# SSD decays from running sums stored as rows and read back for all partitions by DMA, with two of five gate pieces moved into the tile loop

## The chip, the cores and the metric

One core of a Trainium2 chip runs the whole program. The metric is the device time of one execution in microseconds (us), and the number quoted is the median of several runs. The engines are TensorE (PE, with its weight load PEld), VectorE (DVE), ScalarE (ACT), GpSimd (POOL) and the sequencer SyncE (SP), which here only issues DMAs. They run side by side and wait for one another through semaphores.

## The reference

One layer of a streaming encoder in f32: 512 prompt tokens and 8 streams of 16 sample tokens, 640 tokens in all, width 1024. A Mamba-2 branch (SSD) and a sparse attention branch work on the same normed input, are gated and merged, and a mixture of 32 experts follows. The change is in the SSD branch. For each head it needs, over a tile of 128 tokens (a chunk),

```python
a_cum = jnp.cumsum(ak, axis=1)                       # ak = dt * A, one number per token and head
seg = a_cum[:, :, None] - a_cum[:, None, :]
decay = jnp.where(causal, jnp.exp(jnp.where(causal, seg, 0.0)), 0.0)
cb = jnp.einsum('blgn,bsgn->blsg', ck, bk)
y = jnp.einsum('blsg,blsgr,bsgrp->blgrp', cb, decay, xk)
y = y + jnp.einsum('blgn,bgrpn,blgr->blgrp', ck, state, jnp.exp(a_cum))
...
y_ssd = rmsnorm(y_ssd * jax.nn.silu(z), ssm_norm_g)  # over all 2048 channels
```

There are 32 heads in 4 groups of 8. The sum of squares for the last norm runs over all four groups.

## The kernel before

**Tiling.** 640 tokens are five tiles of 128 (`NT` = 5; tiles 0 to 3 prompt, tile 4, `SMP`, the eight streams). The SSD branch runs group by group, g = 0 to 3 (`ssd_pe`, `ssd_act`, `ssd_dve`, and the loops in the GpSimd and SP blocks). Each engine has its own program in a fixed order, written out by hand; what order results between engines comes from semaphores. PSUM has 8 banks of 128 x 512. `plan_banks` and `plan_group` give each use of a bank a key such as ("z", g, j) and take the banks of a pool in turn: `lo` is banks 0 to 3, `hi` 4 to 7. TensorE may fill a bank (`claim`) when its earlier user has read it (`release`), so with four banks in turn each key waits for the reader of the fourth key before it in its pool.

**A group on TensorE** (`ssd_pe`): six products for x, B and C over the prompt (`xbc` 0 to 5, each eight 128 x 128 weights by 512 columns), with the sample tokens' part `xbcS`; between them in the first group the running sums `ac` and totals `ae`, in later groups the squares of the group before (`squares_pe`: ones times zT, four products for the prompt and four for the sample, summed over partitions and channels at once); then the gate products `z` 0 to 3 and, for the sample tokens of all four, `zS`; transposes of the convolution's last rows (`cO`) and of B (`bt`); and the tile loop. The loop has six steps. Step s transposes x of tile s (`xt`), makes C B^T (`cb`) and the segment sums (`sg`, lines 868 to 874: eight matmuls, one per head, whose weights are one column of a broadcast over 128 columns, so that the running sum of the head stands in every partition), and for tile s-1 the state's part (`yi`, line 882), the new state (`st`, line 890) and the output (`yo`, line 896). After it come the eight streams' states (`so`, `s0`, `sn`, `ys`).

**A group on ScalarE** (`ssd_act`): for each of the six products a copy into `raw` (two buffers) and, one step later, the silu of VectorE's convolution result; the silus of z into zT (lines 1328 to 1332); copies of cO and bt; then for each tile eight Relu (line 1352: the running sum of a head minus its value at the own token, in mt), two Exp over mt (line 1358) and four half Exp of the running sums into ebs (lines 1367 and 1368), both from the PSUM bank of `sg`. After the loop: copies of states, the squares of the gated output into zT (line 1380), and the norm's gain (line 1383).

**A group on VectorE** (`ssd_dve`): for each of the six products the convolution (lines 1556 and 1558), with rounds of the attention's top-k between (lines 1963 and 1964); in the fourth of the six also `squares_dve` of the group before (line 1675: sums added into ssrow). In the loop: dt times x (1588), cb times the causal mask (1593), the state and output sums of the tile before (`tile_dve`), and mt times cb (1602).

**GpSimd** copies the convolution's last rows, multiplies xdt by weights (`xw`, line 737), masks B by stream (743), and issues the DMAs of results: conv rows, states (759), and the group's output to `y_spill` (762).

**SP** issues the loads. Weights go through a ring of three slots (`chunks`): a slot is loaded anew when its user, named in `ring.add`, is done; for wz that is `zS`. In a group SP issues, in order, the conv rows, the weights up to wz of the next group, and four loads of 512 KB of states (line 575). At the end of the stage SP waits for the last squares and reloads q (line 586) for the attention. DMAs of one queue are issued in the order of the program; a wait in front of one holds all behind it.

Of the kernel before, what the change touches and what calls it, by code (L numbers as in the profile page):

```python
# [19 lines left out]
P = 128  # L20
# [173 lines left out]
def plan_group(b, g):  # L194
# [18 lines left out]
    b.add(("zS", g), hi)  # L213
# [24 lines left out]
    if g == GROUPS - 1:  # L238
        for c in range(4):
            b.add(("ga", 0, c), lo)  # L240
            if c == 1:
                for i in range(2):
                    b.add(("ss", g, i), hi)
# [3 lines left out]
def hybrid_layer(nc, x_prompt, x_sample, cache_k, cache_v, cache_kidx, state_conv, state_ssm,  # L247
# [39 lines left out]
    with ExitStack() as ctx:  # L287
# [94 lines left out]
        sout = xdt[:, 1, :]  # L382
        cin, cst = a2.take(6, P), a2.take(6, 24)
# [54 lines left out]
        q_spill = nc.dram_tensor("q_spill", (P, KD, TP), F32, kind="Internal").ap()  # L438
        y_spill = nc.dram_tensor("y_spill", (P, 16, T), F32, kind="Internal").ap()
# [44 lines left out]
        def wait_chunk(pe, key):  # L484
# [7 lines left out]
            "ident_ready", "pads_zeroed", "x_squares", "x_var", "x_std", "x_scaled",  # L492
            "a_row_ready", "wl_ready", "wsel_ready", "rel_used",
            "bias_ready", "dt_exp", "a_exp", "a_ready", "raw_zeroed", "raw_ready", "conv_done",
            "xs_ready", "gathered", "bms_ready", "mt_size", "mt_exp", "xw_ready", "mt_ready",
            "y_gated", "y_squares", "y_gained",
            "q_spilled", "y_spilled", "crow_written", "sout_written", "q_back", "vnew_loaded", "y_back",
            "router_loaded", "fin_loaded", "at_exp", "kz_ready", "p_scaled", "ss_var", "ss_std", "m_ready", "hx_squares",
            "hx_var", "hx_std", "hx_scaled", "r_exp_in", "r_exp", "hot_ready", "rows_ready", "at_ready", "at_used",
            "t_full", "t_read", "up_full", "silu_ready", "he_ready", "heT_full", "heT_ready",  # L500
            "dn_full", "dn_read", "xn_stored", "fx_squares", "fx_var", "fx_std",
            "fin_ready", "last_ready", "rms_ready", "fx_scaled", "y_written", "parts_added", "last_chain")}
        w13_loaded = [sem(f"w13_loaded{i}") for i in range(XS)]
        st0_loaded = [sem(f"st0_loaded{i}") for i in range(3)]
        st0_written = [sem(f"st0_written{i}") for i in range(3)]
        w2_loaded = [sem(f"w2_loaded{i}") for i in range(XS)]
# [13 lines left out]
        def _(sp):  # L520
# [41 lines left out]
            for g in range(GROUPS):  # L562
# [6 lines left out]
                chunks(("wz", min(g + 1, GROUPS - 1)) if g + 1 < GROUPS else ("wgb", 0))  # L569
# [11 lines left out]
            wait_read(sp, ("ss", GROUPS - 1, 1))  # L581
# [74 lines left out]
        def _(pool):  # L656
# [59 lines left out]
            for g in range(GROUPS):  # L716
# [39 lines left out]
                for j in range(4):  # L756
# [3 lines left out]
                                   st0[:, u % 3, :, :]).then_inc(st0_written[u % 3], 16)  # L760
                pool.wait_ge(S["y_gained"], g + 1)
# [1505 lines left out]
```

## Time and profile before

| | us |
|---|---|
| median of 3 runs | 1826.1 (1823.59 to 1828.19) |
| the profiled execution | 1830.48 |
| its span in the trace | 1828.7 |
| TensorE busy | 1635.3 |
| VectorE busy | 688.4 |
| ScalarE busy | 457.1 |
| GpSimd busy | 174.7 |

The profile describes one execution on one core. Busy time is summed over the span; what matters for a change is which engine the others wait for in the stage that it touches. A row of a timeline merges neighbouring instructions of a kind: start, duration, engine, line of the kernel, what is written and read, how many, and in brackets the idle time before it and what ended it. An f32 matmul shows as two records. The mean granted clock of TensorE was 0.94 of full speed. The four SSD groups lie between about 213 and 848 us of the span.

### The profile page before, as it was taken

How to read it: one execution, taken by the hardware profiler on the slowest of the kernel's cores; microseconds unless marked ns; L12 is line 12 of the kernel's file. 1: busy time of each engine (PE TensorE's matmuls, PEld its weight loads, DVE VectorE, ACT ScalarE, POOL GpSimd, SP SyncE). 2: the span in 40 equal slices, each digit the busy share in tenths (PEclk: the TensorE clock that was granted, in tenths of full speed). 3: DMA queues.
4: the chain of work that ended last, by engine and by line, in shares of the span. 5: the costliest groups of instructions: out<-in, count | busy, mean ns of one | idle time of the engine just before them, and what ended most of it. 6: DMA issues, size and time to landing. Idle time of an engine off the chain costs nothing. (4 is left out here: it accounts for less than half of the span.)

```text
span 1828.7 us, 19455 instructions
## 1 busy us (share of the span) xinstructions
PE 1635.3 (89%) x7752; PEld 1004.3 (55%) x7752; DVE 688.4 (38%) x1371; ACT 457.1 (25%) x1070; POOL 174.7 (10%) x250
## 2 busy tenths in 40 slices
PE   8998999999899899989998899999999967977770
PEld 5555555755664764655666665655564544544440
DVE  3003283776677469453554450010001243111105
ACT  2005322521621621522554330000000100111112
POOL 4000000200200210120000000000000012322212
PEclk9999999999999999988999999999999977988985
DMA  9010312220322224024003434031223166999964
GB/s 237 23 46 24 128 47 80 80 87 23 101 78 68 83 94 127 1 65 134 1 1 82 116 138 139 1 138 46 47 75 136 35 261 243 414 416 415 414 251 173
DMA packets 109936, 231.67 MB, mean 127 GB/s; under 512 B 30236, under 2 KB 56420, under 8 KB 101012
## 3 DMA queue, kind: packets, MB, share of 16 engines
q1 hardware_dynamic: 98772, 199.28, 31.3%
q0 software_dynamic: 11072, 31.12, 4.8%
q8 instruction: 63, 1.03, 0.2%
q14 instruction: 29, 0.24, 0.0%
HBM read 200.77 MB, written 31.56 MB: 127 GB/s over the span
## 5 line engine op out<-in xcount | busy, mean ns | idle before, releaser
L1044 PE MATMUL psum<-hT,wring 128*128 128x512 f32 (+1 forms) x2176 | 598.3, 439 | 0.0
L1044 PEld LDWEIGHTS psum<-hT,wring 128*128 128x128 f32 x2176 | 335.7, 196 | 258.3 <-issue 258.0
L1048 PE MATMUL psum<-ident,arena 128*128 128x128 f32 (+3 forms) x926 | 148.2, 294 | 45.3 <-DVE arena L1724 7.3
L1406 ACT ACTIVATE arena<-psum 128x512 f32<-128x512 f32 (+7 forms) x200 | 109.4, 569 | 278.3 <-PE psum L1044 168.4
L1048 PEld LDWEIGHTS psum<-ident,arena 128*128 128x128 f32 (+3 forms) x926 | 112.4, 155 | 100.3 <-issue 66.4
L1044 PE MATMUL psum<-arena,wring 128*128 128x512 f32 (+1 forms) x512 | 138.8, 433 | 0.0
L1044 PEld LDWEIGHTS psum<-arena,wring 128*128 128x128 f32 x512 | 77.0, 190 | 61.6 <-issue 61.6
L1255 PE MATMUL psum<-wring,arena 128*64 128x256 f32 x608 | 79.0, 418 | 23.9 <-issue 17.8
L1255 PEld LDWEIGHTS psum<-wring,arena 128*64 128x64 f32 x608 | 52.0, 151 | 46.4 <-issue 24.4
L1202 PE MATMUL psum<-wring,arena 128*128 128x512 f32 x160 | 72.4, 613 | 3.8 <-DVE arena L2022 3.8
L1700 DVE CUSTOM_DVE_ANT_0 arena<-psum,arena 128x256 f32<-128x256 f32 (+3 forms) x64 | 46.6, 729 | 67.9 <-PE psum L960 42.9
L2064 DVE TENSOR_TENSOR arena<-psum,arena 128x128 f32<-128x128 f32 x32 | 9.3, 292 | 165.0 <-ACT arena L1534 152.1
L1044 PE MATMUL psum<-oT,wring 128*128 128x512 f32 (+1 forms) x256 | 69.6, 434 | 0.0
L1963 DVE MAX8 ssq<-arena 128x8 f32<-128x1040 f32 (+3 forms) x80 | 66.6, 833 | 2.1
L1558 DVE SCALAR_TENSOR_TENSOR arena<-arena,pc 128x664 f32<-128x664 f32 x72 | 65.6, 911 | 2.6
L2010 DVE TENSOR_TENSOR arena<-psum,arena 128x512 f32<-128x512 f32 x8 | 5.5, 692 | 159.2 <-PE psum L1044 159.2
L1964 DVE MATCH_REPLACE8 arena<-ssq,arena 128x1040 f32<-128x1040 f32 (+3 forms) x80 | 65.2, 815 | 0.0
L772 POOL MEMSET arena<- 128x2048 f32 x1 | 1.8, 1804 | 645.8 <-DVE arena L2029 645.8
L1271 PE MATMUL psum<-arena 128*64 128x512 f32 x256 | 60.9, 592 | 0.4 <-ACT arena L1536 0.4
L1393 ACT ACTIVATE arena<-psum 128x512 f32<-128x512 f32 x16 | 9.4, 597 | 192.6 <-PE psum L1044 192.6
L1534 ACT ACTIVATE arena<-psum 128x128 f32<-128x128 f32 x32 | 8.9, 277 | 193.2 <-PE psum L1255 180.0
L1044 PEld LDWEIGHTS psum<-oT,wring 128*128 128x128 f32 x256 | 38.8, 191 | 30.6 <-issue 30.6
(324 smaller groups left out, 1928.7 us busy)
## 6 DMA issues: line engine op xcount, KB each, us to landing
wring<-in_w SPq DMA_DIRECT2D x38, 1024.0 KB
arena<-in_w SPq DMA_DIRECT2D x32, 1024.0 KB, 25.5
wring<-in_w_in SPq DMA_DIRECT2D x13, 2048.0 KB, 7.9
hT<-in_w SPq DMA_DIRECT2D x14, 1024.0 KB
oT<-in_w SPq DMA_DIRECT2D x12, 1024.0 KB
arena<-in_state_ssm SPq DMA_DIRECT2D x16, 512.0 KB, 9.1
out<-arena POOLq DMA_DIRECT2D x16, 512.0 KB, 3.9
wring<-in_w_ssm_out SPq DMA_DIRECT2D x4, 2048.0 KB, 14.0
```

Of the source, the lines that this page charges most:

```text
L1044: ins = mm(out, chunk[:, k, m0:m0 + m], rhs(k), start=first and k == 0, stop=last and k == ks - 1)
L1048: return nc.tensor.transpose(out, in_, ident[0:rows, 0:rows])
L1202: ins = mm(o, mrg[:, k, tt * P:(tt + 1) * P], ws[n][:, k, :], start=k == 0, stop=k == KD - 1)
L1255: ins = mm(pbank(2 + e % 2)[h * SLOTS:(h + 1) * SLOTS, 0:FF].rearrange("p (c f) -> p c f", c=2), hgT[:, e % 2, k, :], w13[e % XS][:, :, k, ...
L1271: ins = mm(pbank(4 + e % 2)[m * SLOTS:(m + 1) * SLOTS, :], heT[:, e % 2, k, :], w2s[e % XS][:, k, HD2 * m:HD2 * (m + 1)], start=k == 0, st ...
L1393: release(fn(gate[:, i, j, 0:TP], bank((what, m, j)), ACT.Sigmoid), (what, m, j))
L1406: release(fn(out, in_, ACT.Copy), key)
L1558: ins = stt(out=a, in0=r[:, w:w + 664], scalar=cw_col[:, w, ct:ct + 1], in1=a, op0=ALU.mult, op1=ALU.add)
L1700: release(nc.vector.tensor_tensor_reduce(out=out, in0=scores, in1=bias, scale=-ATT_SCALE, scalar=3.0e38, op0=ALU.add, op1=ALU.min, accum_o ...
L1963: link(nc.vector.max(top8, scores))
L1964: link(nc.vector.match_replace(scores, top8, scores, TAKEN))
L2064: tt_(hetm[:, u % 2], pbank(2 + u % 2)[:, HF:FF], hsil[:, u % 2], ALU.mult).then_inc(S["he_ready"], 1)
```

## The change

The segment sums are made once, in the first group, for all 32 heads as rows (`ar`: heads on partitions, tokens in columns), copied by ScalarE to `arow`, written by DMA to DRAM (`a_rows`), and for each tile of each group read back so that all 128 partitions hold the eight heads' rows (512 KB a tile). They land in `mt`, which with two halves of `raw` for tile 2 makes three places for six halves. ScalarE works on them in place, in a new order: first the half Exps into ebs, then Relu, then Exp. The decays of tiles 0 and 1 are done in the convolution loop (after the fifth and the sixth silu), those of tile 2 ahead of the silu of z3, of tile 3 ahead of that of zS, and of tile 4 last. `z3` is now made in step 0 of the tile loop and `zS` in step 4. SP's weights go up to wbc of the next group, then the five decays, then wz of the next group. The squares are summed over the channels on GpSimd into ssrow, and TensorE sums over the partitions once, at the end of the last group, after the fourth gate product and no longer after the second. Some semaphores are shared (`row_squares`, `row_var`, `row_std`) in place of three sets with the same waits.

```diff
@@ plan_group
-    if g:
-        for i in range(2):
-            b.add(("ss", g - 1, i), hi)
-    else:
+    if g == 0:
         for tt in range(NT):
             b.add(("ac", tt), hi)
             b.add(("ae", tt), hi, readers=2)
+        for i in range(2):
+            b.add(("ar", i), hi)
...
-    for j in range(4):
+    for j in range(3):
         b.add(("z", g, j), lo)
-    b.add(("zS", g), hi)
...
-            for i in range(2):
-                b.add(("sg", g, step, i), hi)
+        if step == 0:
+            b.add(("z", g, 3), lo)
+        elif step == NT - 1:
+            b.add(("zS", g), hi)
@@ tiles
+        arow = ebs.rearrange("p u n -> p (u n)")[0:HEADS, 0:T]
+        mt_f = mt.rearrange("p u n -> p (u n)")
+        def decays(tt, i):
+            return raw[:, i, 3:515] if tt == 2 else mt[:, 2 * (tt % 3) + i, :]
+        def decays_load(g, tt):
+            return (2, g) if tt == 2 else (tt % 3, 2 * g + tt // 3)
...
+        a_rows = nc.dram_tensor("a_rows", (NT, HEADS, P), F32, kind="Internal").ap()
@@ SP, in each group
-                chunks(("wz", min(g + 1, GROUPS - 1)) if g + 1 < GROUPS else ("wgb", 0))
+                chunks(("wbc", g + 1) if g + 1 < GROUPS else ("wga", 0))
+                if g == 0:
+                    wait_read(sp, ("ar", 0))
+                    wait_read(sp, ("ar", 1))
+                    sp.dma_start(a_rows.rearrange("t h l -> h t l"), arow.rearrange("h (t l) -> h t l", t=NT)) \
+                        .then_inc(S["arow_written"], 16)
+                    sp.wait_ge(S["arow_written"], 16)
+                for tt in range(NT):
+                    if tt == 2:
+                        sp.wait_ge(S["conv_done"], 6 * (g + 1))
+                        sp.wait_ge(S["gathered"], 6 * (g + 1))
+                    elif tt > 2:
+                        wait_full(sp, ("yo", g, tt - 3))
+                    elif g:
+                        wait_full(sp, ("yo", g - 1, tt + 3))
+                    at = (tt % 3) * 1024
+                    dst = raw[:, :, 3:515] if tt == 2 else mt_f[:, at:at + 1024].rearrange("p (i n) -> p i n", i=2)
+                    sp.dma_start(dst, a_rows[tt, HG * g:HG * (g + 1), :].rearrange("(o i h) l -> o i (h l)", o=1, i=2)
+                                 .broadcast_to([P, 2, 512])).then_inc(decays_loaded[decays_load(g, tt)[0]], 16)
+                chunks(("wz", g + 1) if g + 1 < GROUPS else ("wgb", 0))
...
-            wait_read(sp, ("ss", GROUPS - 1, 1))
+            sp.wait_ge(S["squares_added"], GROUPS)
@@ GpSimd, in each group, after the states' writes and ahead of y_spill
+                pool.wait_ge(S["y_squares"], g + 1)
+                for j in range(4 if g else 3):
+                    a, b = (ssrow, zT[:, j, :]) if g else (ssrow if j else zT[:, 0, :], zT[:, j + 1, :])
+                    ins = nc.gpsimd.tensor_tensor(ssrow, a, b, ALU.add)
+                    if j < (3 if g else 2):
+                        link(ins)
+                ins.then_inc(S["squares_added"], 1)
@@ ssd_pe
-            if g:
-                squares_pe(pe, g - 1)
-            else:
+            if g == 0:
...
+                for i in range(2):
+                    o = claim(pe, ("ar", i))
+                    for tt in range(4 * i, min(4 * i + 4, NT)):
+                        ins = mm(o[0:HEADS, (tt - 4 * i) * P:(tt - 4 * i + 1) * P], av[:, tt, :],
+                                 (cum_p if tt < SMP else cum_s)[:], start=True, stop=True)
+                    filled(ins, ("ar", i))
...
-            for j in range(4):
+            for j in range(3):
                 o = claim(pe, ("z", g, j))
...
-                    for i in range(2):
-                        o = claim(pe, ("sg", g, tt, i))
-                        for h in range(4):
-                            hd = HG * g + 4 * i + h
-                            ins = mm(o[:, h * P:(h + 1) * P], av[:, tt, hd:hd + 1].broadcast_to([P, P]),
-                                     (cum_p if tt < SMP else cum_s)[:], start=True, stop=True)
-                        filled(ins, ("sg", g, tt, i))
                 if step == 0:
+                    o = claim(pe, ("z", g, 3))
+                    filled(product(o, w, 3 * P, P, prompt, TP), ("z", g, 3))
                     continue
+                if step == NT - 1:
+                    o = claim(pe, ("zS", g))
+                    for j in range(4):
+                        ins = product(o[:, j * P:(j + 1) * P], w, j * P, P, sample, P)
+                    filled(ins, ("zS", g))
...
-            pe.wait_ge(S["y_squares"], g + 1)
+            pe.wait_ge(S["squares_added"], g + 1)
...
-                for j in range(4):
-                    ins = mm(o[:, 0:b - a], ones[:], zT[:, j, a:b], start=j == 0, stop=j == 3)
-                filled(ins, ("ss", g, i))
+                filled(mm(o[:, 0:b - a], ones[:], ssrow[:, a:b], start=True, stop=True), ("ss", g, i))
@@ ssd_act
+                if j >= 5:
+                    decays_act(act, g, j - 5, fn)
             if g:
-                wait_full(act, ("ss", g - 1, 1))
-            for j in range(4):
+                act.wait_ge(S["squares_added"], g)
+            for j in range(3):
                 wait_full(act, ("z", g, j))
...
+            decays_act(act, g, 2, fn)
+            wait_full(act, ("z", g, 3))
+            release(fn(zT[:, 3, 0:TP], bank(("z", g, 3)), ACT.Silu), ("z", g, 3))
+            decays_act(act, g, 3, fn)
+            wait_full(act, ("zS", g))
+            release(fn(zT[:, :, TP:T], bank(("zS", g)).rearrange("p (j q) -> p j q", j=4), ACT.Silu), ("zS", g))
+            decays_act(act, g, 4, fn)
...
+        def decays_act(act, g, tt, fn):
+            k = NT * g + tt
+            b, n = decays_load(g, tt)
+            act.wait_ge(decays_loaded[b], 16 * (n + 1))
+            if tt >= 2:
+                wait_read(act, ("yo", g, tt - 2))
+            elif g:
+                wait_read(act, ("yo", g - 1, tt + 3))
+            for i in range(2):
+                dst = ebs[:, k % 2, 2 * i * P:2 * (i + 1) * P].rearrange("p (j l) -> p j l", l=P)
+                src = decays(tt, i).rearrange("p (j o l) -> p o j l", o=2, l=P)
+                fn(dst[0:HP], src[0:HP, 0], ACT.Exp)
+                ins = fn(dst[HP:P], src[HP:P, 1], ACT.Exp)
+            ins.then_inc(S["ebs_ready"], 1)
+            act.wait_ge(S["ebs_ready"], k + 1)
+            for i in range(2):
+                for h in range(4):
+                    hd = HG * g + 4 * i + h
+                    m = decays(tt, i)[:, h * P:(h + 1) * P]
+                    ins = fn(m, m, ACT.Relu, bias=acv[:, tt, hd:hd + 1], scale=-1.0)
+                ins.then_inc(S["mt_size"], 1)
+            for i in range(2):
+                act.wait_ge(S["mt_size"], 2 * k + i + 1)
+                m = decays(tt, i)
+                fn(m, m, ACT.Exp, scale=-1.0).then_inc(S["mt_exp"], 1)
```

## Rows read from the trace of the kernel before

**Rows 1.** The page's first part: busy time of each engine, share of the span, instructions.

```profile
PE 1635.3 (89%) x7752; PEld 1004.3 (55%) x7752; DVE 688.4 (38%) x1371; ACT 457.1 (25%) x1070; POOL 174.7 (10%) x250
```

**Rows 2.** Timeline of TensorE, third group: start, us, engine, line, operation, count, [idle before].

```profile
546.92 4.49 PE L947 MATMUL psum<-arena,ones 128*128 128x512 f32 x16
...
611.46 1.16 PE L872 MATMUL psum<-cum_p,arena 128*128 128x128 f32 x8 [2.94 <-ACT arena L1368]
...
619.85 1.09 PE L896 MATMUL psum<-arena 128*64 128x128 f32 x16
...
621.59 1.95 PE L872 MATMUL psum<-cum_p,arena 128*128 128x128 f32 x16
623.38 1.06 PE L882 MATMUL psum<-arena 128*128 128x128 f32 x8
...
625.22 1.09 PE L896 MATMUL psum<-arena 128*64 128x128 f32 x16
...
634.99 1.98 PE L896 MATMUL psum<-arena 128*64 128x128 f32 x16 [3.30 <-DVE arena L1602]
```

**Rows 3.** Timeline of ScalarE, third group.

```profile
585.97 0.72 ACT L1322 ACTIVATE arena<-arena,pc 128x512 f32<-128x512 f32 x1 [10.15 <-DVE arena L1558]
...
589.35 0.60 ACT L1330 ACTIVATE arena<-psum 128x512 f32<-128x512 f32 x1 [1.40 <-PE psum L1044]
...
603.36 0.60 ACT L1332 ACTIVATE arena<-psum 128x512 f32<-128x512 f32 x1 [6.55 <-PE psum L1044]
...
606.12 2.17 ACT L1352 ACTIVATE arena<-psum,arena 128x128 f32<-128x128 f32 x8 [0.77 <-PE psum L872]
608.31 1.28 ACT L1358 ACT_TABLE_LOAD   x1
...
622.68 2.17 ACT L1352 ACTIVATE arena<-psum,arena 128x128 f32<-128x128 f32 x8 [0.75 <-PE psum L872]
```

**Rows 4.** Groups of VectorE's instructions: count, busy us, mean ns, idle before.

```profile
L1602 DVE TENSOR_TENSOR arena<-arena 128x512 f32<-128x512 f32 x40 | 25.7, 685 | 17.8 <-ACT arena L1358 17.8
```

**Rows 5.** Timeline of VectorE, third group.

```profile
562.47 1.00 DVE L1675 TENSOR_TENSOR arena<-arena,psum 128x512 f32<-128x512 f32 x2
```

**Rows 6.** Windows: us, busy of each engine, then PE's clock, DMA share, GB/s.

```profile
633.00:640.50 7.50, 5.51 (x30) 4.69 (x31) 3.10 (x5) 1.79 (x3) 3.07 (x6) 0.54 0.07 19
```

**Rows 7.** Timeline of ScalarE, first and second group.

```profile
276.82 0.60 ACT L1406 ACTIVATE arena<-psum 128x512 f32<-128x512 f32 x1 [3.66 <-PE psum L1044]
...
311.35 0.60 ACT L1332 ACTIVATE arena<-psum 128x512 f32<-128x512 f32 x1 [6.55 <-PE psum L1044]
...
442.42 0.72 ACT L1322 ACTIVATE arena<-arena,pc 128x512 f32<-128x512 f32 x1 [14.62 <-DVE arena L1558]
...
456.18 0.60 ACT L1332 ACTIVATE arena<-psum 128x512 f32<-128x512 f32 x1 [6.55 <-PE psum L1044]
```

**Rows 8.** DMA issues of 563 to 583 us: count, KB each, median us to landing.

```profile
wring<-in_w_in SPq DMA_DIRECT2D x2, 512.0 KB, 4.6
```

**Rows 9.** DMA issues of the whole span.

```profile
arena<-in_x_prompt SPq DMA_DIRECT2D x8, 512.0 KB, 4.0
```

**Rows 10.** Groups of GpSimd's instructions.

```profile
L737 POOL TENSOR_TENSOR arena<-arena 128x512 f32<-128x512 f32 x20 | 20.8, 1041 | 220.9 <-DVE arena L1588 220.9
```

**Rows 11.** Timeline of ScalarE at the end of the fourth group.

```profile
819.24 2.98 ACT L1383 ACTIVATE oT<-oT,pc 128x640 f32<-128x640 f32 x4
```

**Rows 12.** Timeline of TensorE where the attention starts.

```profile
848.51 0.83 PE L960 MATMUL psum<-arena,oT 128*128 128x128 f32 x6
```

**Rows 13.** DMA issues of 600 to 625 us.

```profile
wring<-in_w_in SPq DMA_DIRECT2D x1, 2048.0 KB, 7.8
arena<-in_state_ssm SPq DMA_DIRECT2D x3, 512.0 KB, 9.2
```

**Rows 14.** Groups of ScalarE's instructions.

```profile
L1352 ACT ACTIVATE arena<-psum,arena 128x128 f32<-128x128 f32 x160 | 43.5, 383 | 11.5 <-PE psum L872 11.3
```

More of the change, by code:

```diff
@@ L505, in hybrid_layer @@
         st0_written = [sem(f"st0_written{i}") for i in range(3)]
+        decays_loaded = [sem(f"decays_loaded{i}") for i in range(3)]
         w2_loaded = [sem(f"w2_loaded{i}") for i in range(XS)]
@@ L834, in ssd_pe @@
             w = wait_chunk(pe, ("wz", g))
-            for j in range(4):
+            for j in range(3):
                 o = claim(pe, ("z", g, j))
                 filled(product(o, w, j * P, P, prompt, TP), ("z", g, j))
-            o = claim(pe, ("zS", g))
-            for j in range(4):
-                ins = product(o[:, j * P:(j + 1) * P], w, j * P, P, sample, P)
-            filled(ins, ("zS", g))
             pe.wait_ge(S["gathered"], 6 * (g + 1))
@@ L1297, in ssd_act @@
                     fn(w2v, w2v, ACT.Exp).then_inc(S["a_exp"], 1)
+                    copy(("ar", 0), arow[:, 0:512], bank(("ar", 0))[0:HEADS, :])
+                    copy(("ar", 1), arow[:, 512:T], bank(("ar", 1))[0:HEADS, 0:P])
+                if j == 0 and g:
+                    wait_full(act, ("yo", g - 1, 2))
                 if j < 6:
@@ L1325, in ssd_act @@
                        bias=cb_col[:, ct:ct + 1]).then_inc(S["xs_ready"], 1)
+                if j >= 5:
+                    decays_act(act, g, j - 5, fn)
             if g:
-                wait_full(act, ("ss", g - 1, 1))
-            for j in range(4):
+                act.wait_ge(S["squares_added"], g)
+            for j in range(3):
                 wait_full(act, ("z", g, j))
                 release(fn(zT[:, j, 0:TP], bank(("z", g, j)), ACT.Silu), ("z", g, j))
-            wait_full(act, ("zS", g))
-            release(fn(zT[:, :, TP:T], bank(("zS", g)).rearrange("p (j q) -> p j q", j=4), ACT.Silu), ("zS", g))
             if g:
@@ L1385, in ssd_act @@
             if g == GROUPS - 1:
+                act.wait_ge(S["squares_added"], GROUPS)
                 gate_act(act, "ga", 0, fn)
+        def decays_act(act, g, tt, fn):
[21 more added lines that the diff above has]
+                act.wait_ge(S["mt_size"], 2 * k + i + 1)
+                m = decays(tt, i)
+                fn(m, m, ACT.Exp, scale=-1.0).then_inc(S["mt_exp"], 1)
         def gate_act(act, what, m, fn):
@@ L1568, in ssd_dve @@
                         release(tt_(w2v[:, tt, :], bank(("ae", tt))[:, 0:HEADS], acv[:, tt, :], ALU.subtract), ("ae", tt))
-                if j == 3 and g:
-                    squares_dve(dve, g - 1)
                 a, b = TOP_UPTO[g], TOP_UPTO[g + 1]
@@ L1600, in ssd_dve @@
                         dve.wait_ge(S["mt_exp"], 2 * k + i + 1)
-                        m = mt[:, (2 * k + i) % 4, :].rearrange("p (h l) -> p h l", h=4)
+                        m = decays(tt, i).rearrange("p (h l) -> p h l", h=4)
                         tt_(m, m, cbs[:, k % 2, :].rearrange("p (o l) -> p o l", o=1).broadcast_to([P, 4, P]), ALU.mult) \
@@ L1604, in ssd_dve @@
             k = NT * g + SMP
-            for i in range(2):
-                wait_read(dve, ("sg", g, SMP, i))
+            dve.wait_ge(S["ebs_ready"], k + 1)
             wait_read(dve, ("yo", g, SMP))
@@ L1642, in tile_dve @@
                 wait_full(dve, ("yi", g, tt))
-                for i in range(2):
-                    wait_read(dve, ("sg", g, tt, i))
+                dve.wait_ge(S["ebs_ready"], k + 1)
                 wait_read(dve, ("yo", g, tt - 1))
@@ L1671, in squares_dve @@
                 src = bank(("ss", g, i))[:, 0:b - a]
-                if g == 0:
-                    ins = nc.vector.tensor_copy(ssrow[:, a:b], src)
-                else:
-                    ins = tt_(ssrow[:, a:b], ssrow[:, a:b], src, ALU.add)
-                release(ins, ("ss", g, i))
+                release(nc.vector.tensor_copy(ssrow[:, a:b], src), ("ss", g, i))
                 wait_read(dve, ("ss", g, i))
```

81 lines of the change are left out of this document (26 added, 55 removed).

## The prediction

> **What bounds the kernel now.** The page's first part comes first: TensorE is busy 89% of the span, every other engine under 40% [rows 1]. So I read the change from TensorE's side, in the four SSD groups, which it alone touches (about 213 to 848 us). The timeline of TensorE in the third group (g = 2) shows why that stage is TensorE's: its rows follow one another without idle time except for 2.94 us at the first tile and 3.30 us at the last [rows 2]. A middle tile costs 5.37 us from one L896 group to the next (619.85 to 625.22), of which the segment sums (L872) hold 1.79 us (621.59 to 623.38) [rows 2]. ScalarE waits 0.75 us a tile for L872 [rows 3], so its own work (eight Relu, two Exp, four half Exp) is 5.37 - 0.75 = 4.6 us. VectorE has seven operations of 0.69 us a tile [rows 4] and a smaller one, about 5 us. Three engines are therefore nearly level inside the tile loop, and taking work from one of them cannot give its full price.
>
> **What is removed.** 160 segment-sum matmuls, eight a tile in 16 records (621.59 [rows 2]): 20 tiles by 1.79 us is 35.8 us. The squares: a row of 4.49 us a group (546.92 [rows 2]), of which 0.17 overlaps with its neighbour, so 4.32, and 17.3 us in all; two matmuls (about 1.0 us: four records, two of 0.43 and two of 0.11) stay at the very end. Added on TensorE: five 32-row running sums, 128 columns each, about 1.2 us once by the spacing in L872. Net 50.9 us of TensorE work. That is the upper bound; what follows is how much of it ScalarE's new order gives back.
>
> **The third group, step by step, on the trace's own clock.**
> (1) When the loop can start. Before it needed z(0..3) and the sample part; two of these five, z3 and zS, now lie inside the loop. They are 14.0 us (589.35 to 603.36 [rows 3]). With 4.3 us of squares gone, TensorE comes to the transposes at 603.2 - 18.3 = 584.9. But these wait for the last silu of the convolution, which started on ScalarE at 585.97 [rows 3], when VectorE's convolution ended (it has top-k rounds between its six parts). That VectorE chain starts at the first product of the group and doesn't shorten, except for 1.0 us of adding squares [rows 5]. So the silu ends at 585.0 + 1.1 = 586.1. Up to here the removed squares are worth nothing: another engine is late.
> (2) The first hand-over. ScalarE now does the decays of tile 1 right after this silu, and only then z0, z1, z2 and the copies of cO and B. The bank of cb(0) is free when cO(0) has been copied (four banks in turn: cO0, cO1, bt0, bt1, cb0), and that of z3 when z0 has been read. In front of it: a load of the Exp table 1.28 [rows 3], the decays 4.75 (the 4.6 of a tile, with 0.15 for a new wait on its own half Exps), a load of the Silu table 1.28, three silus 1.6, the copy 0.6: 586.1 + 9.5 = 595.6. TensorE is there at 587.5. It stands idle for 8.1 us, where before it had 2.94.
> (3) Then xt/cb and z3. z3 is 6.87 us at full clock. After an idle time of only 3.3 us the granted clock was 0.54 over 633 to 640.5 [rows 6], that is mostly at 1.2 GHz; after 8 us I expect the same. Over such a stretch the loss is between 1.7 and 3.4 us by how much of 7.5 us was slow; I take 2.3. z3 ends at 605.0.
> (4) Tiles 0 to 2. Step 1 is 2.7 us on TensorE (xt, cb, state, output, from the rows of 0.95 to 1.1 us [rows 2]): 607.7. VectorE reads that output (0.7), and only then may ScalarE begin tile 2: 608.4 + 4.75 = 613.2. VectorE has 1.3 (tile 1's product), 1.0, four operations of 0.69 and 1.3 more: 614.7. The output of tile 2 is done at 615.6. The steps are now VectorE's 5 us, not TensorE's 3.6: the 1.79 us saved per tile is given back here but for 0.4.
> (5) Tile 4. xt, cb and zS on TensorE: 615.6 + 0.7 + 7.15 = 623.5. TensorE then has tile 3 (2.9 us) and is out of work at 626.4. ScalarE must turn zS (0.6), load the Exp table (1.28), do the half Exps, Relus and the first Exp of tile 4 (4.2), VectorE the product (0.7): 630.2. So 3.8 us idle, in place of the 3.30. The output takes 1.98 us at the slow clock, as in the row of before: 632.2, against 634.99 + 1.98 = 636.97 [rows 2]. **Saved: 4.8 us** of a removed 8.9 + 4.3 us.
>
> **The other groups.** The fourth I take like the third: 4.8. In the second the last silu stands only 13.8 us before zS's (442.42, 456.18 [rows 7]) against 17.4 in the third [rows 3]: everything in (2) to (5) hangs on it, so 3.6 less: 1.2. In the first the silu is early, but the running sums go out to DRAM and come back: SP issues the write behind the 1 MB of the next B and C weights, when their slot is free (the product read at 276.82 [rows 7], 278.0 with the added matmuls). Their 4.6 us to landing [rows 8], 2.7 for the write (80 KB, an estimate below the 4.0 of a 512 KB load [rows 9]) and 4.0 for the first load give 289.3 for tile 0's decays, 294.0 for their end, 296.3 for the last silu, and by the sum of (2) 305.8 for cO. From there 36.6 us as in the third: 342.4, against 311.35 [rows 7] + 33.6 = 345.0 (33.6 is the third group's way from zS's silu to 636.97). Saved 2.6.
>
> **The end.** GpSimd adds four 128 x 640 parts. Its row of 1041 ns for 512 elements a partition [rows 10] puts one at 1.3, four at 5.2 us. In the first three groups they fall into VectorE's idle time after the gated product. In the last the squares are done when the gain starts, 819.24 [rows 11], the sum at 824.5, and TensorE has gates to do until 837: hidden. y_spill, now behind the adds, and with it q's reload, come about 1 us later than in the trace; the attention starts at 848.5 - 3.3 = 845.2 [rows 12], and a 2 MB load from 829.5 with 7.8 us to landing [rows 13] leaves 8 us for VectorE's two short copies of the keys. 17.3 less 1.0 on paper, 3.3 here.
>
> **What is hidden.** Twenty more loads of 512 KB. Tile 2's comes after the last convolution and is wanted 20 us later; tile 3's is issued at 607.7 and wanted at 616, tile 4's 4 us later and wanted at 625. A 512 KB load of states took 9.2 us even behind 2 MB [rows 13]; alone I take the 4.0 of the x rows. Bounds: nothing, and 5 us once in the first group if a broadcast load takes 8. The loads that they displace matter more: z's weights for the next group (slot free only when zS is done) now stand before the states on SP's queue. 2 MB took 7.8 us to land [rows 13] and I put the first state 2 us later: 623.5 + 9.8 = 633.3, wanted at 633.1 (after the 0.9 us of state transposes). Cost zero now; up to 4 us a group if the loop goes quicker than I sum.
>
> **The sum.** 2.6 + 1.2 + 4.8 + 4.8 + 3.3 = 16.7 us. The profiled execution took 1830.48 us, 4.4 above the median of 1826.1; its stages after 848 us shift whole. 1830.5 - 16.7 = 1813.8; at the median, 1809.4.
>
> **A rule on the tables.** ScalarE pays 1.28 us a load in the trace, and nothing else: the Relus end at 606.12 + 2.17 = 608.29, the load starts at 608.31 [rows 3]. By the trace's price a group has four loads on the path, 5.1 us, already in the sum. The Trainium skill, "ScalarE: Activation LUTs", What ACT_TABLE_LOAD costs, adds about 1.38 us of drain to every switch, and its rule to batch by table set speaks against this change, which goes from Silu to Exp five times a group where it went once. By the page's figure the drains would be 5.5 us a group more, 22 in all: 1831 as an estimate. The row shows no such gap.
>
> **Rivals.**
> A, TensorE stays the bound: the waits of (2) and (5) don't arise because ScalarE is far enough ahead. For it: ScalarE is busy only 25% of the span [rows 1]. Against: its order is serial. 50.9 us less: 1775.
> B, ScalarE's serial piece is longer than I sum; this one ends slower. Place: the decays of tile 1 ahead of cO's copy, and those of tile 4 after zS. Price: a Relu alone lasts 383 ns [rows 14] and eight come to 3.1 instead of 2.17; with two half-clock stretches of full length (1.1 more each) and the waits between the three sub-steps at 0.5 each, 6.0 us a group (1.8, 2.2 and 2.0), 24 in all: 1833. It makes the kernel slower than before from 4.2 us a group on.
> C, a switch of tables costs twice its row, because the engine must run empty first and the loads of before stood where that didn't show: four more times 1.28 a group, 20.5 us: 1830. Against it: the load of 608.31 stood in a full stretch and had no gap [rows 3].
> D, the exchange is even: the idle time grows by just what was removed, or the reloaded rows in the first group and the states behind z's weights take back 12 us: 1821 to 1830.
>
> **Chances.** My forecast 0.54 (own range 1800 to 1819); A or half of it 0.12; B 0.16; C 0.04; D 0.14. The range 1791 to 1830 leaves out A's far end and most of B. A measurement of this kernel tells 0.3% (5.5 us) from no change: faster is my forecast and A, 0.66; same C and D, 0.18; slower B, 0.16.
>
> **What would show it.** TensorE idle for about 8 us ahead of the first cb or z3 in groups 2 to 4, released by ScalarE; a second idle time of about 4 us before the last tile's output; steps of 5 us in between with VectorE full; L872 gone; ten table loads a group; the squares' sum of GpSimd done before the gates are. Wrong if TensorE runs through (A), if the state transposes wait for DMA, or if the last silu of the convolution isn't what ends the wait before the loop.

## The result: 1.3% slower, 1848.8 us against 1825.4, and the profile after

| | before | after |
|---|---|---|
| median, four runs each on one chip | 1825.44 (1823.59 to 1828.19) | 1848.8 (1847.72 to 1852.39) |
| the profiled execution | 1830.48 | 1852.39 |
| its span | 1828.7 | 1850.6 |

The ratio is 1.0127, 95% interval [1.0109, 1.0146]. I had predicted 1809.4 us in a range of 1791 to 1830: the wrong direction, and outside the range. The first part of the page of after answers to [rows 1]:

```profile
span 1850.6 us, 18747 instructions
PE 1591.5 (86%) x7382; PEld 961.8 (52%) x7382; DVE 683.1 (37%) x1365; ACT 509.8 (28%) x1104; POOL 194.3 (10%) x265
```

TensorE is busy 43.8 us less than in [rows 1] and the span is 21.9 us longer: its idle time grew by 65.7 us. The waits of TensorE by line and releaser, in total, times, longest, of after:

```profile
PE psum L917 <- ACT arena L1381: 34.6, 4, 8.6
PE psum L902 <- ACT arena L1451: 29.9, 4, 8.7
PE psum L931 <- DVE arena L1645: 19.2, 4, 4.8
```

Each of the three comes once a group. L902 (cb of tile 0) and L931 (output of tile 4) are the two waits that the prediction has, at 8.1 and 3.8 us. The largest, L917, the state's part `yi` of tile 1, it doesn't have. (`yi` is what the state that earlier tiles left adds to a tile's output.) The timeline of TensorE of after in the third group, against [rows 2]:

```profile
601.30 1.20 PE L1081 MATMUL psum<-ident,arena 128*128 128x128 f32 x9 [0.34 <-ACT arena L1360]
611.17 0.79 PE L902 MATMUL psum<-arena 128*128 128x128 f32 x2 [8.66 <-ACT arena L1451]
611.75 8.94 PE L1077 MATMUL psum<-hT,wring 128*128 128x512 f32 x16
...
622.14 1.09 PE L931 MATMUL psum<-arena 128*64 128x128 f32 x16
...
632.69 2.05 PE L917 MATMUL psum<-arena 128*128 128x128 f32 x8 [8.64 <-ACT arena L1381]
634.53 1.79 PE L925 MATMUL psum<-arena 128*128 128x512 f32 x2
...
637.99 1.06 PE L917 MATMUL psum<-arena 128*128 128x128 f32 x8
638.88 1.02 PE L925 MATMUL psum<-arena 128*128 128x512 f32 x2
...
641.58 7.31 PE L1077 MATMUL psum<-hT,wring 128*128 128x128 f32 x64
...
656.48 1.95 PE L931 MATMUL psum<-arena 128*64 128x128 f32 x16 [4.80 <-DVE arena L1645]
```

z3 (611.75) is done at 620.7. Why is its silu (L1381) so late? The timeline of ScalarE of after says it:

```profile
610.54 1.49 ACT L1451 ACTIVATE arena<-psum 27x512 f32<-27x512 f32 x4
624.12 1.28 ACT L1418 ACT_TABLE_LOAD   x1 [12.10 <-DVE oT L1704]
...
627.15 2.45 ACT L1426 ACTIVATE arena<-arena 128x128 f32<-128x128 f32 x8
629.50 1.13 ACT L1431 ACTIVATE arena<-arena 128x512 f32<-128x512 f32 x2
630.65 1.28 ACT L1381 ACT_TABLE_LOAD   x1
631.95 0.60 ACT L1381 ACTIVATE arena<-psum 128x512 f32<-128x512 f32 x1
```

In ScalarE's program the decays of tile 2 stand ahead of the silu of z3. They overwrite ebs, so they wait for VectorE's read of yo(0), the copy in L1704. ScalarE stands idle for 12.10 us, the last 3.4 of them with z3 ready, then does table load, decays and table load, and only at 632.55 is the bank of z3 free. The keys of the low banks go in turn z3, xt1, yo0, xt2, yi1: the next user of z3's bank is yi(1). So tile 1's state part waits for the silu of a gate piece whose result is wanted only behind the loop. Then it and the row behind it run at half speed: 2.05 and 1.79 us where the same rows a step later take 1.06 and 1.02. The windows of after, with the granted clock behind the busy times, show 0.53 there, that is the 1.2 GHz level, after 8.64 us of idle time; z3 behind the first idle time had 0.76:

```profile
611.00:620.50 9.50, 9.33 (x18) 4.32 (x19) 1.59 (x3) 1.02 (x4) 0.00 (x0) 0.76 0.00 0
632.50:636.30 3.80, 3.61 (x12) 2.26 (x12) 0.69 (x1) 0.04 (x1) 0.00 (x0) 0.53 0.00 0
```

The price is 8.64 us of idle time and 0.99 + 0.77 us of slow rows, 10.4 us a group and 41.6 in all. With the 16.7 us of saving that I had summed this makes +24.9 us, against +21.9 in the profiled execution.

The end of the stage, of after: GpSimd's sum of squares, and then, on TensorE's timeline, the two products over the partitions and the start of the attention, which answers to [rows 12]:

```profile
842.13 5.49 POOL L793 TENSOR_TENSOR arena<-arena 128x640 f32<-128x640 f32 x4 [8.71 <-ACT arena L1397]
```

```profile
859.88 1.24 PE L981 MATMUL psum<-arena,ones 128*128 128x512 f32 x4
...
868.11 0.83 PE L993 MATMUL psum<-arena,oT 128*128 128x128 f32 x6
```

### The profile page after: what moved, and what is told of

It reads as the page before. It is cut to its first block and busy times, and to the rows that moved or that the text cites. A ratio compares the mean times of both kernels' runs of the same rounds, so it can differ in the third digit from the quotient of the medians.

```text
span 1850.6 us, 18747 instructions
## 1 busy us (share of the span) xinstructions
PE 1591.5 (86%) x7382; PEld 961.8 (52%) x7382; DVE 683.1 (37%) x1365; ACT 509.8 (28%) x1104; POOL 194.3 (10%) x265
## 5 line engine op out<-in xcount | busy, mean ns | idle before, releaser
L1451 ACT ACTIVATE arena<-psum 128x512 f32<-128x512 f32 (+5 forms) x202 | 109.8, 568 | 239.4 <-PE psum L1077 140.4
```

The costliest lines, as they stand in the source:

```text
L1451: release(fn(out, in_, ACT.Copy), key)
```

## Experiments

Theory T: the loss is a chain: VectorE's read of yo(0), then the decays of tile 2, then the silu of z3, then the bank for yi(1). Rivals: the table loads (R1), the reloads from DRAM and other traffic (R2), the decays as such being too much serial work on ScalarE (R3). Each ratio is to the kernel before on the same chip. The rows come from several chips, so compare ratios and not medians. The last three columns are of each kernel's one profiled execution: the length of the SSD stage, from the transposes of the first convolution rows (212.84 in before) to the start of the attention (848.51); the length of the attention over the prompt behind it, from the first to the last of the products of [rows 12]; and the table loads of ScalarE in the stage.

| kernel | median us | ratio [95%] | stage us | attention us | table loads |
|---|---|---|---|---|---|
| before | 1825.44 | 1 | 635.7 | 118.7 | 9 |
| e4, squares alone | 1807.33 | 0.9885 [0.9863, 0.9907] | 621.3 | 110.4 | 9 |
| e3, squares and rows, gates before the loop | 1777.82 | 0.9713 [0.9673, 0.9754] | 587.3 | 110.4 | 25 |
| after | 1848.8 | 1.0127 [1.0109, 1.0146] | 654.0 | 118.7 | 41 |
| e1, after, silu of z3 ahead of decays 2 | 1820.24 | 0.9951 [0.9934, 0.9969] | 626.4 | 118.7 | 33 |
| e5, after, decays 2 without their wait | 1806.84 | 0.9864 [0.983, 0.9897] | 617.8 | 110.4 | 41 |
| e2, e1 and decays 1 behind z0 to z2 | 1784.43 | 0.9763 [0.9742, 0.9784] | 588.5 | 118.7 | 33 |
| e6, e2 and silu of zS last | 1779.76 | 0.9717 [0.9686, 0.9748] | 585.6 | 118.7 | 26 |
| e7, e6 and states ahead of z's weights | 1762.47 | 0.9626 [0.9597, 0.9655] | 565.1 | 118.7 | 26 |
| e9, e7 and decays 2 without their wait | 1761.79 | 0.9632 [0.9613, 0.965] | 565.5 | 118.7 | 26 |
| e8, e3 and decays 2 without their wait | 1777.24 | 0.9691 [0.9653, 0.9728] | 585.7 | 118.8 | 25 |
| e10, e8 and states ahead of z's weights | 1768.75 | 0.9655 [0.9618, 0.9691] | 581.7 | 118.7 | 25 |

The attention is not touched by any edit, and yet it has two lengths. From 5 us after its start TensorE runs for 20 us at a granted clock of 0.50 (1.2 GHz) in nine of these executions, and at 1.00 (2.4 GHz) in those of e3, e4 and e5. The windows of e2 and of e3, whose attention starts at 802.40 and 802.45 us behind the same kind of products and has the same 2.35 us of idle time near its start:

```profile
807.40:827.40 20.00, 20.00 (x65) 11.28 (x66) 8.38 (x50) 8.66 (x38) 0.00 (x0) 0.50 0.01 2
807.45:827.45 20.00, 18.70 (x96) 11.58 (x96) 12.56 (x69) 13.11 (x53) 0.00 (x0) 1.00 0.01 2
```

What decides between the two isn't known. So some 8 us, 0.45% of the time, can lie between two kernels' ratios without a cause in the change; the stage's length is free of it, but it is from one execution of each.

**e1: the order of two calls on ScalarE.**

```diff
-            decays_act(act, g, 2, fn)
             wait_full(act, ("z", g, 3))
             release(fn(zT[:, 3, 0:TP], bank(("z", g, 3)), ACT.Silu), ("z", g, 3))
+            decays_act(act, g, 2, fn)
```

> The changed kernel with two blocks of ScalarE's program exchanged: the silu of z3 stands ahead of tile 2's decays. Theory (the bank): z3 and yi(1) share a PSUM bank, z3 is read only after tile 2's decays, and these wait for tile 0's output to be read, so TensorE stands 8.6 us before yi(1) in each group and runs on at the slow clock for about 2 us. Then this wait goes, yo(2) waits 1 to 2 us instead, and a group is 9 us shorter: 1811 us (1805 to 1817). Rival 1 (ScalarE's decays and table loads as a whole are the bound, yi(1) is only the first place where it shows): the wait moves to yo(2), 3 us a group at most: 1837. Rival 2 (the rows read back by DMA arrive late): no difference, 1849.

The wait of L917 for z3's bank is gone, with as many reloads as in after. The table loads are not as many: with the silu out from between them, the decays of tiles 2 and 3 follow each other on one table, 33 loads for 41. The eight that are gone are 10.3 us at most, so this run alone does not settle R1; e5 does. TensorE in the third group of e1:

```profile
588.03 1.20 PE L1081 MATMUL psum<-ident,arena 128*128 128x128 f32 x9 [0.34 <-ACT arena L1360]
597.89 0.80 PE L902 MATMUL psum<-arena 128*128 128x128 f32 x2 [8.66 <-ACT arena L1451]
...
615.34 1.16 PE L917 MATMUL psum<-arena 128*128 128x128 f32 x8 [0.66 <-DVE arena L1695]
...
618.11 1.17 PE L931 MATMUL psum<-arena 128*64 128x128 f32 x16 [0.75 <-DVE arena L1645]
...
634.82 1.97 PE L931 MATMUL psum<-arena 128*64 128x128 f32 x16 [4.80 <-DVE arena L1645]
```

From the first transpose to the end of the last output it is 48.8 us (588.03 to 636.79), in after 57.1 (601.30 to 658.43). The two ratios differ by 0.0176, 32 us; the stage is 27.6 us shorter. At 1820 us the kernel is still some 9 us slower than I expected of it, and outside the range given. ScalarE in e1:

```profile
607.78 0.60 ACT L1380 ACTIVATE arena<-psum 128x512 f32<-128x512 f32 x1 [9.03 <-PE psum L1077]
611.17 1.28 ACT L1418 ACT_TABLE_LOAD   x1 [2.79 <-DVE oT L1704]
```

The silu of z3 runs as soon as z3 is there, and the wait for yo(0) is still 2.79 us long behind it.

**e5: the other link of the same chain.** Tile 2's decays don't wait for VectorE; the silu of z3 stays behind them. The wait guards the half Exps of tile 0, and these have no reader: a prompt starts without a state, so there is no yi of tile 0 (VectorE copies its output where it adds for the others). It can go without a race.

```diff
-            if tt >= 2:
+            if tt >= 3:
                 wait_read(act, ("yo", g, tt - 2))
-            elif g:
+            elif g and tt < 2:
                 wait_read(act, ("yo", g - 1, tt + 3))
```

> The changed kernel, ScalarE's order as it is, but tile 2's decays don't wait for tile 0's output to be read (tile 0 has no part that reads ebs, so the buffer is free). Theory (the bank of z3 is read late because tile 2's decays stand before it and wait): they now run beside z3's product, the silu of z3 follows at once, the 8.6 us before yi(1) go without the exchange of the first experiment; 1814 us (1808 to 1822). Rival (it was the exchange itself, one pair of table loads fewer, that helped): 1840 or more.

The same idle time is gone (none before yi(1); 0.65 us before yi(2), where e1 has 0.66), with all 41 table loads and all reloads of after, and the stage is 36.3 us shorter than that of after: R1 and R2 fall as the cause of the loss. The kernel is faster than e1 by 0.9%, 16 us. Of the 17.0 us between the two profiled executions 8.7 are in the stage, where ScalarE does tile 2's decays in the 9.03 us in which e1 leaves it waiting for z3; 8.3 are the attention's clock. Either link broken ends the loss: it is the chain, not the order alone and not the wait alone.

**e4 and e3: the parts without the gate pieces.** e4 is before with GpSimd's sum of squares alone. e3 is after with z3 and zS made ahead of the loop again:

```diff
-            for j in range(3):
+            for j in range(4):
                 o = claim(pe, ("z", g, j))
...
+            o = claim(pe, ("zS", g))
...
-                if step == 0:
-                    o = claim(pe, ("z", g, 3))
-                if step == NT - 1:
-                    o = claim(pe, ("zS", g))
```

> The kernel before with the squares' sum alone moved to GpSimd and one product at the end. Theory: ahead of the loop TensorE is the late one here (the last silu is 13 to 17 us early), so all of it counts: 4 times 4.3 less 1.1 is 16.2 us: 1809 us. My prediction's step (1) says that the same edit is worth nothing once the gates are in the loop. Rival (GpSimd's sums delay VectorE or the conv rows, or the convolution bounds already): 1825.

> The changed kernel with z3 and zS back ahead of the tile loop on TensorE and ScalarE (and their banks planned there): only the rows by DMA and the squares on GpSimd remain of the change. Theory: tiles 0 and 1 get their decays beside 14 us of gate products, no bank of a gate stands in the loop, and of 51 us removed from TensorE nearly all is won: 1776 us (1768 to 1788), the loop 23 us instead of 33. Rival (rows by DMA cost what they save: ScalarE's half Exps, Relus and Exps in place last longer, and each load waits for an output three tiles back): 1815 to 1830.

Squares alone are worth 1.15%, about 21 us, but 14.4 us in the stage, for 16.2 expected; its profiled execution had another 8.3 us from the attention's clock, which are not the squares'. That leaves little that the GpSimd adds could cost. Rows and reloads in addition are worth 0.9885 - 0.9713 = 1.7%, 31 us, and 34.0 in the stage, of the 35.8 of matmuls removed. All reloads and all decays of after are in e3, so R2 and R3 fall. The whole loss goes with the two gate pieces: 1.0127 against 0.9713, about 76 us (66.8 in the stage), at the place where they were put and with ScalarE's order left as it was. TensorE of e3: all of its waits in the loop of the third group, and the last one of the fourth group's:

```profile
585.93 1.10 PE L919 MATMUL psum<-arena 128*128 128x512 f32 x2 [1.29 <-POOL arena L763]
...
593.20 1.16 PE L911 MATMUL psum<-arena 128*128 128x128 f32 x8 [0.75 <-DVE arena L1687]
...
595.97 1.17 PE L925 MATMUL psum<-arena 128*64 128x128 f32 x16 [0.74 <-DVE arena L1637]
...
599.47 1.16 PE L911 MATMUL psum<-arena 128*128 128x128 f32 x8 [1.52 <-DVE arena L1687]
...
606.26 1.63 PE L925 MATMUL psum<-arena 128*64 128x128 f32 x16 [3.74 <-DVE arena L1637]
...
742.22 1.17 PE L925 MATMUL psum<-arena 128*64 128x128 f32 x16 [3.74 <-DVE arena L1637]
```

There is no first hand-over at all: 14 us of z3 and zS ahead of the loop are what ScalarE's decays of tile 1 were hidden behind. Moving these pieces into the loop took the cover from one wait (8.66) and made another (8.64).

**e2: the first hand-over.** In e1 the decays of tile 1 are moved from behind the sixth silu to behind the silus of z0 to z2 and the copies of cO and B.

```diff
-                if j >= 5:
-                    decays_act(act, g, j - 5, fn)
+                if j == 5:
+                    decays_act(act, g, 0, fn)
...
+            decays_act(act, g, 1, fn)
```

> As the one before, and tile 1's decays moved behind the silus of z0 to z2 and the copies of cO and B. Theory (the bank): the 8.7 us before cb(0) are tile 1's decays with two table loads in front of the read of cO's bank; they go too, tile 1's decays fit beside z3's 6.9 us, about 10 us a group less than the one before: 1772 us (1764 to 1782). Rival (ScalarE's total work in the loop bounds): the decays of tile 1 now push tile 2's back by 6.5 us and nothing is won: as the one before.

```profile
572.25 0.49 PE L902 MATMUL psum<-arena 128*128 128x128 f32 x2 [0.70 <-ACT arena L1452]
572.58 7.03 PE L1077 MATMUL psum<-hT,wring 128*128 128x512 f32 x16
...
606.68 1.97 PE L931 MATMUL psum<-arena 128*64 128x128 f32 x16 [4.81 <-DVE arena L1646]
```

These are the same rows of e2: 8.66 became 0.70, and z3 fell from 9.26 in e1 to 7.03. The gain is 1.9%, 34 us, and 37.9 in the stage, near to 4 x (7.96 + 2.23) = 41. At 1784 us the kernel is just above the range that I gave, 1764 to 1782. It has the 33 table loads of e1, so R1 has no part in this step.

**e6 and e7: the last wait, and what it uncovers.** e6 puts the decays of tile 4 ahead of zS's silu. e7 has SP issue the three state loads ahead of the last piece of z's weights, which wait for zS.

```diff
-                chunks(("wz", g + 1) if g + 1 < GROUPS else ("wgb", 0))
...
+                    if j == 3:
+                        chunks(("wz", g + 1) if g + 1 < GROUPS else ("wgb", 0))
```

> The second experiment (tile 1's decays behind z0 to z2, z3's silu ahead of tile 2's), and the silu of zS behind tile 4's decays. Theory: the 4.8 us and about 1 us of slow clock before tile 4's output go, but the states' loads stand behind 2 MB of z weights that wait for zS on SP's queue: the first state lands some 10 us after zS and is now wanted 4.5 us after it, so about 5 of 5.8 us are given back: 1782 us (1776 to 1786). Rival (the states are in time): 1761.

> As the one before, and three of the four loads of states issued ahead of the z weights of the next group. Theory: the states are no longer late, and the whole 5.8 us a group is won: 1761 us (1755 to 1768). Rival (the states are in time already): the same as the one before.

TensorE of e6, then of e7 (third group):

```profile
604.59 1.19 PE L931 MATMUL psum<-arena 128*64 128x128 f32 x16 [1.90 <-DVE arena L1646]
610.06 1.94 PE L1081 MATMUL psum<-ident,arena 128*128 128x128 f32 x8 [3.23 <-DMA arena<-in_state_ssm]
```

```profile
592.07 1.17 PE L932 MATMUL psum<-arena 128*64 128x128 f32 x16 [1.90 <-DVE arena L1647]
```

e6 shortened the wait from 4.81 to 1.90 and runs the output at full speed (1.19 for 1.97), yet it gained only 0.5%, with intervals that overlap, and 2.9 us in the stage: the states, late by 2.5 us only in the fourth group of after, now come 3.23 us late here and 2.7 to 3.6 us in the other groups. The issues on SP's queue, of e6, then of e7:

```profile
599.94 0.38 SPq L538 DMA_DIRECT2D wring<-in_w_in  x1
600.37 7.49 SPq L604 DMA_DIRECT2D arena<-in_state_ssm  x3
```

```profile
574.44 4.28 SPq L605 DMA_DIRECT2D arena<-in_state_ssm  x3
...
587.42 0.37 SPq L538 DMA_DIRECT2D wring<-in_w_in  x1
```

With the states ahead of the weights, e7 is 0.9% faster than e6, 17 us, and 20.5 in the stage.

**e8, e9, e10: what the freed wait is worth elsewhere, and where the gates should be.**

> The third experiment (gates ahead of the loop) with the needless wait of tile 2's decays dropped. Theory: ScalarE's three decays in the loop (5.1 us each, 15.4 in all, from 589.0 to 605.8) bound that loop; they start up to 5 us earlier, and the last wait of 3.7 us goes: 1765 us (1758 to 1772). Rival (VectorE's 5 us a tile bound the loop): 1774.

> e7 with the decays of tile 2 no longer waiting for VectorE's read of yo(g,0). In e7 they stand behind the silus of z0 to z2 and z3, so ScalarE comes to them only some us after that read could matter. My theory: the loop's steps are then bound by the wait of tile 3's decays for the read of yo(g,1), as in e8, where the freed wait moved one tile on (3.28 us) and the SSD stage became 1.9 us shorter in all: 1759 to 1762. Rival, every wait of the decays counts once in each group: in e7 the wait before tile 2 is then worth its full 2 to 3 us a group, about 10 us: 1752.

> e8 (gates before the loop, tile 2 without its wait) with the three state loads issued ahead of z's weights of the next group. In e8 no state is late, because zS comes early and z's weights were in before the states were wanted. Theory: no change from the order, 1768 to 1778. Rival: the states' loads were what spread e8's runs between 1768 and 1782, and with them first all runs are at the low end, 1766. It also says which place of z3 and zS is the better one with the same order of loads: against e7 (inside the loop, 1762) it should be 5 to 15 us slower, if the gates inside the loop fill TensorE's idle time at the steps; not slower, if what e7 won came from the loads alone.

e8 missed its forecast: 1777 us, for 1758 to 1772. The rival had 1774, with VectorE's 5 us a tile as the bound of the loop, and the trace is on its side. Without the wait of tile 2's decays ScalarE waits with tile 3's, for VectorE's read of yo(1), and VectorE itself has no idle time from 583.64 to 605.08. Its products of tiles 1, 2 and 3 begin 4.9 to 5.0 us apart. ScalarE of e8, then VectorE:

```profile
593.80 0.42 ACT L1410 ACTIVATE arena<-arena 64x256 f32<-64x256 f32 x1 [3.28 <-DVE oT L1694]
```

```profile
588.71 1.28 DVE L1637 TENSOR_TENSOR arena<-arena 128x512 f32<-128x512 f32 x2
593.63 1.28 DVE L1637 TENSOR_TENSOR arena<-arena 128x512 f32<-128x512 f32 x2
598.61 1.29 DVE L1637 TENSOR_TENSOR arena<-arena 128x512 f32<-128x512 f32 x2
```

e9 against e7 confirms that a wait taken from ScalarE there is worth nothing: no difference (0.9632, 0.9626; the stage 565.5 and 565.1), where the rival had 10 us.

Where should the gates be? The ratios don't tell: e10 is 0.3% behind e7 with overlapping intervals, and e2 against e3 (0.9763, 0.9713) leans the other way. The stages do, for one execution each. e2 and e3 are equal (588.5 and 587.3); the attention's clock can make the rest. With the silu of zS last and the states first, the gates inside the loop are better: 565.5 us in e9 against 581.7 in e10, 16 us where I had expected 5 to 15 (ScalarE's order differs with the place). In the loop TensorE waits 11.7 us in the four groups of e9 and 26.9 in those of e10, before the products and sums of VectorE and GpSimd. The runs of e3, e8 and e10 spread over 13 to 17 us, those of e7 and e9 over 3 to 6. The rival's cause for it, the states' loads, falls, since e10 has them first. Its runs stand in pairs, 1760 and 1762 us at a mean granted clock of 0.951, 1775 and 1777 at 0.940 and 0.941; the attention's two lengths could be 8 us of that, but the first pair left no trace, and the cause stays open. e7 and e9 are the best versions, 3.7% faster than before.

## Why the prediction was wrong, step by step

The end of the last output of each group, and the start of the attention, in the profiled executions (from the L896 and L931 rows, [rows 2, 12]), as increments against before. The first column also holds what lies ahead of the stage, which began 1.2 us later in after and 2.2 later in e1:

| | group 0 | 1 | 2 | 3 | end |
|---|---|---|---|---|---|
| before, us | 345.5 | 489.8 | 637.0 | 783.7 | 848.5 |
| predicted | -2.6 | -1.2 | -4.8 | -4.8 | -3.3 |
| after | +9.0 | +9.6 | +2.9 | +3.6 | -5.4 |
| e1 | +1.3 | +2.6 | -4.1 | -2.6 | -4.3 |

The sum of after is +19.6 and of e1 -7.1, of the prediction -16.7. So the chain, as e1 breaks it, holds 26.7 of the 36.3 us, and the other 9.6 are sizes and the later start. The stage of e5 is 17.9 us shorter than before's. That it comes near to the 16.7 is luck: e5 does tile 2's decays under z3, which the prediction didn't have.

- **Step (4) failed.** It says "VectorE reads that output (0.7), and only then may ScalarE begin tile 2", and sums the steps as "VectorE's 5 us". It has the wait itself right, but not what stands behind it in ScalarE's queue, the silu of z3, nor who takes that silu's bank. Step (2) follows the banks in turn up to cb0 and z3 and stops there; one turn further is yi(1). It asks when z3 gets its bank, and never who gets it after z3. The two rows of yi(1) and the state, for which I took no idle time, cost 8.64 us of waiting and 1.76 of slow clock.
- **Step (1) holds.** TensorE's transposes wait 0.34 us for the last silu of the convolution (601.30), for 1.2 in the sum. That the removed squares are worth nothing up to there is argued and not tried: by (1)'s own sum TensorE with its squares would come 3.1 us behind that silu, but it would still stand in the 8.66 us that follow.
- **Step (2) holds, a little short.** 8.66 us for 8.1. The decays take 5.2 (602.56 to 607.77: four half Exps of 0.41 to 0.43, the Relus 2.44, two Exps 1.13), not 4.75: the Relus, now from SBUF, take 2.44 for eight where those from PSUM took 2.17 [rows 3].
- **Step (3) holds.** z3 took 8.94 us; I had 6.87 + 2.3 = 9.17.
- **Step (4) even without the chain** is too short: in e1 the output of tile 2 is done 31.3 us after the first transpose (619.28), predicted 29.5. VectorE's waits (0.66 and 0.75) are small, but tile 2's decays begin at 612.46, behind a wait of 2.79 us and then a table load (611.17) which the sum doesn't have. Its "VectorE's 5 us" a step is what the rows of e8 show.
- **Step (5) was mis-sized:** 4.80 for 3.8. The silu and the table load (649.54) were in the sum; from the first half Exp (650.84) to VectorE's product (655.63) it is 4.8 us for the 4.2 summed, and the rest is in small steps between the engines.
- **The first group's reload holds.** Tile 0's rows landed for ScalarE at 289.68; the prediction said 289.3. The timeline of ScalarE of after:

```profile
289.68 0.42 ACT L1418 ACTIVATE arena<-arena 64x256 f32<-64x256 f32 x1 [6.34 <-DMA arena<-a_rows]
```

- **The reading of before** has a gap. Step by step it says that TensorE's rows follow one another but for 2.94 and 3.30 us; the trace of before has a third wait in the same group, 0.80 us at 616.11 for ScalarE (L1368). It enters no term of the sum.
- **The end** gave more than the 3.3 summed, 5.4. GpSimd's four adds took 5.49 us (predicted 5.2) and were over at 847.6, 12 us ahead of their reader: hidden, as said.
- **What is hidden:** the reloads took 3.8 us to land, and no engine's wait is put down to them outside the first group. The warning that the states fall late "if the loop goes quicker" came true in e6, at 2.7 to 3.6 us a group.

Of the rivals, B came nearest by its sign and for a wrong reason (it had ScalarE's work too long at the two places that I knew, not a third place). C is refuted: all ten table loads of a group are there and cost their 1.28 us; between the end of the Exp row and the load there is a gap of 0.02 us (629.50 + 1.13 = 630.63, load at 630.65). The 1.38 us of drain per switch of the Trainium skill, "ScalarE: Activation LUTs", What ACT_TABLE_LOAD costs, doesn't show in this trace either.

## What to carry to other kernels

When an operation on one engine is moved behind a wait, go through everything that stands behind it in that engine's program and ask of each not only who needs its result but who takes over the bank or buffer that it frees; with banks in turn, follow the keys all the way round the pool. A piece of work that is moved "out of the way" may be the cover under which another engine does its serial part: look what ScalarE did during these 14 us before taking them away. When two kernels differ by less than a per cent, compare the length of the changed stage too: here a stage that no edit touched moved the total by 8 us. And an order which the waits of the old kernel kept harmless (states behind z's weights) has to be looked at again each time that a wait goes.

## What the runs showed of the hardware

- The place of a table load depends on the wait behind it. In after the loads for the decays of tiles 2 and 3 start after the wait has ended (624.12, and another at 638.58 behind a wait of 6.03 us), so the 1.28 us is on the path. For the last silu of the convolution in e3 the load comes ahead of the wait, at 564.44 with the silu at 568.04. Those behind the wait have two things to wait for, VectorE's read and the load from DRAM, the other has one; whether that is the cause was not tried. It is worth 1.28 us at each place:

```profile
564.44 1.28 ACT L1353 ACT_TABLE_LOAD   x1
568.04 0.72 ACT L1353 ACTIVATE arena<-arena,pc 128x512 f32<-128x512 f32 x1 [2.32 <-DVE arena L1595]
...
589.03 1.28 ACT L1410 ACT_TABLE_LOAD   x1 [4.88 <-DVE oT L1696]
```

- The same products can run at either clock level in two executions. The attention over the prompt, which no edit touched, took 118.7 us where TensorE had 0.50 over 20 us near its start, and 110.4 where it had 1.00, with the same 2.35 us of idle time near its start (e2 and e3).
- Idle time of TensorE is charged twice. After 8.64 us idle the next rows ran at a granted clock of 0.53, and 1.76 us were lost on top; after 1.90 us idle (e6) the output took 1.19 in place of the 1.95 to 1.98 after 4.8 us. The length of the wait alone doesn't say it: after 3.74 us idle in e3 the same output took 1.63 in the third group and 1.17 in the fourth, after 3.30 us in [rows 2] 1.98.
